# Layer 1's recurrence: inverse matrices kept as 64-column chunk blocks, products as 64x64 blocks

## The chip, the cores and the metric

The kernel runs on one core of a Trainium2 chip. The metric is device time in microseconds of one execution. TensorE is PE in the profile (PEld is its weight load), VectorE is DVE, ScalarE is ACT, GpSimd is POOL.

## The reference

One inference step of a two-layer trunk, for a prompt of 256 tokens and 8 samples of 4 tokens, all in fp32. Layer 0 (SSD heads, sliding-window attention, dense feed-forward) and the mixture of experts behind layer 1 are not touched. The part that matters is the RWKV-7 time mixing of layer 1, 16 heads of width 64:

```python
def step(S, inp):
    r_t, w_t, k_t, v_t, a_t, b_t = inp
    sa = jnp.einsum('bhvk,bhk->bhv', S, a_t)
    S = S * w_t[:, :, None, :] + sa[..., None] * b_t[:, :, None, :] + v_t[..., None] * k_t[:, :, None, :]
    return S, jnp.einsum('bhvk,bhk->bhv', S, r_t)
S1, y = lax.scan(step, wkv0.astype(f32), (tm(r), tm(decay), tm(k), tm(v), tm(-kk), tm(kk * a)))
```

## The kernel before

The scan over 256 tokens is done in four chunks of 64. Inside a chunk the tokens depend on each other through a strictly lower triangular 64x64 matrix per head; the kernel builds the inverse of (1 - that matrix) by doubling, in 6 levels (blocks of 1, 2, 4, ... 32). Two chunks are done at a time as one 128x128 matrix with a block-diagonal mask, so half of each such matrix is zeros. A group g (0 to 3) is a pair of chunks (g // 2) and one half of the heads (8 heads, g % 2).

The order of the work is written out by hand in the list `core`, which every engine walks; `step(name, ...)` appends a step and gives it PSUM banks. The steps of a group:

- X (banks for two row halves): the triangular products of the group, 4 pairs of heads x 2 halves, each with 64 rows contracted and 128 columns. VectorE masks them into `Xt` (L1994).
- M0: VectorE makes the first inverse (level 0 entries plus identity) into `Mti` (L2003, L2005), two ops for each half q of the heads.
- T (g, lv, q): 4 transposes on TensorE (L2777), copied by ScalarE (L1313) from `Mi` to `Mti` (level 0: from `Mti` to `Mi`).
- LY (g, lv, q): 4 products `Xl` x `Mi` of 128x128 (mm, L2317), copied by ScalarE to `Yi` (L1313). `Xl` is `Xt` masked for the level, made by GpSimd (L935, `masked_rows`).
- LM (g, lv, q): 4 products `Mti` x `Yi`, added to `Mi` by VectorE (L2022).
- A (g, p): the score matrices of the pair p of heads, 2 products of 128 columns and 2 of 256; VectorE masks them into `A3` (L2012). There are four A steps a group: behind LM of levels 2 and 4, and around LM of level 5.
- QZ, QU, QY, QS (g, cc): the state part for one chunk cc of the group before, between the steps of the levels: QZ and QU at levels 1 and 3, QY and QS at levels 2 and 4. They use the diagonal blocks of `Mi` and `A3`. QZ opens with products of shape 128*64, the rest of it and QU use one position of the array (64x64); QY and QS alternate between two output halves. ScalarE copies QZ, QU and QY; VectorE updates the state (L2032, L2039).
- Group 0 has no state part; Rv, BO and VT (other projections and transposes) lie between its steps, and VT in group 2.

A level of a later group is therefore, on TensorE: LY 0, T 0, LY 1, T 1, (QZ, or QY and QS), LM 0, LM 1, (QU at levels 1 and 3; A at 2 and 4; X and M0 of the next group at 4). T is that of the level before, and there is none in level 1.

PSUM has 8 banks used in turn: step number modulo 8 gives the bank, `take(g)` waits until the bank's last holder is read, `bank_full` and `bank_free` are its two semaphores. The helper `mm` (L2317) is one matmul call; for fp32 it is two LDWEIGHTS and two MATMUL instructions in the trace, so a step of 4 products has 8.

## Time and profile before

| | |
|---|---|
| median of 3 runs | 1682.53 us (1679.84 to 1685.45) |
| span of the profiled execution | 1682.8 us |
| PE busy in it | 1650.8 us (98%) |
| PEld, DVE, ACT, POOL busy | 1372.4, 1172.6, 915.0, 145.1 us |
| the recurrence's four groups | from about 636 to 797 us |

All numbers are of one profiled execution. A busy PE is not PE at its peak: matmuls are pipelined and their ends are modelled, so the starts of the weight loads tell the pace better than the busy time. "[0.33 <-issue]" behind a row is idle time ahead of it in which the engine waited for nothing that the profile shows.

### The profile page before, as it was taken

The numbers are of one execution on the slowest core, as the hardware profiler recorded it, in microseconds if no ns is written. First come the engines' busy times: TensorE is split into PE (matmuls) and PEld (weight loads), VectorE is DVE, ScalarE is ACT, GpSimd is POOL, SyncE is SP. The second block draws the span as 40 slices with busy tenths as digits, with TensorE's granted clock in tenths as the row PEclk, the third lists the DMA queues.
The fourth block names the chain that finished last, engine by engine and source line by source line (L and its number), as shares of the span: only waits on it lengthen the run. The fifth ranks groups of instructions, "written<-read, shape, count | busy, mean of one in ns | idle before, by whom it ended". The sixth has DMA issues, their size and how long they took to land.

```text
span 1682.8 us, 25536 instructions
## 1 busy us (share of the span) xinstructions
PE 1650.8 (98%) x9976; PEld 1372.4 (82%) x9976; DVE 1172.6 (70%) x1512; ACT 915.0 (54%) x1190; POOL 145.1 (9%) x180
## 2 busy tenths in 40 slices
PE   9999999999999999999999999999999999999999
PEld 7766687999997778998866887878788887878787
DVE  4663732766767645443556979798887979898897
ACT  3352532533427425333435767687776767687774
POOL 1104000000000023222032000000000000000101
PEclk9999889999999999999899999999999999999999
DMA  8922433544423220000156989798997979898993
GB/s 342 390 109 100 201 150 152 225 150 151 150 95 145 101 100 1 2 2 2 58 200 245 427 332 428 313 419 355 377 412 319 428 307 424 347 386 350 380 426 127
DMA packets 41096, 405.02 MB, mean 241 GB/s; under 512 B 4784, under 2 KB 5072, under 8 KB 11664
## 3 DMA queue, kind: packets, MB, share of 16 engines
q1 hardware_dynamic: 34336, 372.64, 54.9%
q0 software_dynamic: 6672, 31.14, 4.6%
q8 instruction: 63, 1.03, 0.2%
q14 instruction: 25, 0.20, 0.0%
HBM read 379.49 MB, written 26.30 MB: 241 GB/s over the span
## 4 chain that ended last, share of the span: by engine, by line
PE 90%; DVE 4%; DMA 2%; ACT 2%; issue 1%; POOL 0%; DVEq 0%; ACTq 0%; SPq 0%; POOLq 0%
PE ps L2317 86%; DMA ring<-in_moe_w 1%; PE ps L3089 1%; PE ps L2777 1%; DVE rest_ring L2124 1%; DMA arena<-in_moe_w 1%; PE ps L2725 1%; DVE arena L1668 0%; ACT arena L1251 0%; DVE arena L1681 0%; ACT arena L1264 0%; PE ps L3042 0%; PE ps L2519 0%; DVE arena L1756 0%; POOL ring L924 0%
## 5 line engine op out<-in xcount | busy, mean ns | idle before, releaser
L2317 PE MATMUL ps<-head,hsel 128*128 128x512 f32 x1408 | 458.1, 397 | 2.8 <-DVE rest_ring L2124 2.8
L2317 PEld LDWEIGHTS ps<-head,hsel 128*128 128x128 f32 x1408 | 264.6, 188 | 61.4 <-DVE rest_ring L2124 7.8
L2124 DVE TENSOR_TENSOR rest_ring<-ring,head 128x2048 fp32r<-128x2048 f32 x128 | 291.1, 2285 | 13.7 <-ACT head L1403 13.7
L2317 PE MATMUL ps<-arena,ring 128*128 128x288 f32 (+9 forms) x1408 | 255.8, 347 | 1.2 <-ACT arena L1257 1.2
L1403 ACT ACTIVATE head<-ring 128x2048 fp32r<-128x2048 f32 x128 | 243.1, 1913 | 20.7 <-DMA ring<-in_moe_w 20.6
L2317 PEld LDWEIGHTS ps<-arena,ring 128*128 128x128 f32 (+4 forms) x1408 | 199.3, 189 | 52.4 <-issue 7.7
L2317 PE MATMUL ps<-rest_ring,hsel 128*128 128x512 f32 x512 | 199.8, 390 | 0.0
L2317 PE MATMUL ps<-head,actT_split 128*128 128x512 f32 x512 | 169.1, 394 | 7.4 <-issue 5.6
L2317 PE MATMUL ps<-rest_arena,head 128*128 128x288 f32 x704 | 174.8, 296 | 0.0
L2317 PE MATMUL ps<-rest_arena,rest_ring 128*128 128x288 f32 x528 | 155.6, 295 | 0.0
L2317 PE MATMUL ps<-h,ring 128*128 128x288 f32 (+2 forms) x624 | 133.5, 371 | 1.8 <-DVE h L1513 1.8
L2317 PEld LDWEIGHTS ps<-h,ring 128*128 128x128 f32 (+2 forms) x624 | 99.6, 176 | 35.3 <-issue 8.9
L2317 PEld LDWEIGHTS ps<-rest_arena,head 128*128 128x128 f32 x704 | 122.6, 188 | 0.1
L2317 PEld LDWEIGHTS ps<-head,actT_split 128*128 128x128 f32 x512 | 96.1, 188 | 31.6 <-issue 8.3
L2118 DVE TENSOR_TENSOR rest_ring<-ring,head 128x2048 fp32r<-128x2048 f32 x48 | 109.7, 2285 | 9.7 <-ACT head L1398 9.6
L2317 PE MATMUL ps<-arena 64*64 64x64 f32 (+11 forms) x1194 | 103.2, 289 | 9.8 <-DVE arena L1701 4.0
L2124 DVE TENSOR_TENSOR rest_arena<-arena,head 128x1024 fp32r<-128x1024 f32 (+1 forms) x64 | 110.3, 1751 | 2.0 <-ACT head L1403 1.7
L2317 PEld LDWEIGHTS ps<-rest_ring,hsel 128*128 128x128 f32 x512 | 96.5, 188 | 18.2
L2317 PE MATMUL ps<-hsel,head 128*128 128x288 f32 x352 | 103.9, 295 | 0.0
L1579 DVE TENSOR_TENSOR x<-x,ps 128x288 f32<-128x288 f32 x110 | 48.2, 452 | 77.7 <-PE ps L2317 77.4
L1403 ACT ACTIVATE head<-arena 128x1024 fp32r<-128x1024 f32 (+1 forms) x64 | 92.5, 1486 | 14.7 <-DMA arena<-in_moe_w 14.5
L2317 PE MATMUL ps<-rest_ring,actT_split 128*128 128x512 f32 x256 | 99.8, 390 | 0.0
(387 smaller groups left out, 2476.0 us busy)
## 6 DMA issues: line engine op xcount, KB each, us to landing
ring<-in_moe_w SPq DMA_DIRECT2D x64, 2048.0 KB, 12.2
ring<-in_moe_w SPq DMA_DIRECT2D x64, 1024.0 KB, 8.2
arena<-in_moe_w SPq DMA_DIRECT2D x24, 2048.0 KB, 11.3
arena<-in_moe_w SPq DMA_DIRECT2D x24, 1024.0 KB, 6.9
ring<-in_ffn_w SPq DMA_DIRECT2D x11, 2048.0 KB, 7.6
ring<-in_ffn_w SPq DMA_DIRECT2D x11, 1024.0 KB, 4.9
moe_rows<-arena POOLq DMA_DIRECT2D x1, 6656.0 KB, 34.0
ring<-in_w_in SPq DMA_DIRECT2D x2, 3072.0 KB, 13.0
```

Of the source, the lines that this page charges most:

```text
L1403: A(mhead[c % 2][:, o:o + w], mslot[s][:, o:o + w], ACT.Copy).then_inc(sem("gu_head"), 1)
L1579: V.tensor_tensor(x[:, m, :], x[:, m, :], bank(g)[:, 0:T], ALU.add).then_inc(freesem(g), 1)
L2118: V.tensor_tensor(mrest[s][:, GU:SLOT], mslot[s][:, GU:SLOT], down_head(c).bitcast(F32), ALU.subtract).then_inc(sem("dn_split"), 1)
L2124: V.tensor_tensor(mrest[s][:, o:o + w], mslot[s][:, o:o + w], mhead[c % 2][:, o:o + w].bitcast(F32), ALU.subtract).then_inc(sem("gu_split" ...
L2317: return nc.tensor.matmul(o, l, r, start=start, stop=stop, skip_group_check=skip)
L2725: ins = nc.tensor.transpose(b[0:rows, i * P:(i + 1) * P], src[:, 4 * hf + i, t0:t0 + rows], ident)
L2777: ins = nc.tensor.transpose(b[:, n * P:(n + 1) * P], (Mi if lv else Mti)[gg % 2][:, 4 * q + n, :], ident)
L3089: ins = nc.tensor.transpose(turned(c)[:, u * P:(u + 1) * P], actm[c % 2][:, u * P:(u + 1) * P], ident)
```

## The change

The matrices `Mi`, `Xt`, `Xl` and `A3` lose their zero halves. Tokens of chunk 0 stay in partitions 0 to 63 and those of chunk 1 in 64 to 127, but a head now has 64 columns and not 128. `Mti` and `Yi` are laid out by pairs of heads: partitions by the head's parity, columns by chunk. Every product of a head and chunk is a 64x64 block, and four of them are issued in turn at the four (row half, column half) positions of the array: (0,0), (1,1), (0,1), (1,0). Products from different row halves go to different banks, so X, A, LY and LM each hold two neighbouring banks with one semaphore (`stage(..., pair=True)`, which rounds the bank up to an even one); LY and LM have 128 columns of each bank.

- LY, LM: 8 products of 64x64 instead of 4 of 128x128. One ScalarE copy or VectorE add of 256 columns over both banks instead of 512.
- T: 2 transposes of 128x128 (two heads in one) instead of 4. Level 0 too goes from `Mi` to `Mti`.
- X: both the product and its transpose, 2 x 16 products of 64x64, instead of 8 of 128 columns. M0 is made from the transposed half straight in PSUM (two VectorE ops of 512 columns), and LY and LM of level 1 wait for M0 alone.
- A: two steps a group (behind LM of levels 2 and 4) of two pairs of heads each, 8 products of 64 columns and 8 of 128; one VectorE op of 768 columns.
- The constant table is narrower (64-column masks).

```diff
-            n = {"X": 2, "A": 2, "M0": 0, ...}.get(name, 1)
-            stage((name, *which), n)
+            n = {"X": 2, "A": 2, "LY": 2, "LM": 2, "M0": 0, ...}.get(name, 1)
+            stage((name, *which), n, pair=name in ("X", "A", "LY", "LM"))
...
                 if lv == 5:
-                    step("A", g, 2)
...
-                    step("A", g, 3)
...
                 elif name == "T":
-                    out_of(g, (Mti if lv else Mi)[gg % 2][:, 4 * q:4 * q + 4, :], bank(g).rearrange("p (h t) -> p h t", t=P))
+                    out_of(g, Mti[gg % 2][:, 2 * q:2 * q + 2, :], bank(g)[:, 0:256].rearrange("p (k t) -> p k t", t=P))
                 elif name == "LY":
-                    out_of(g, Yi[:, 4 * q:4 * q + 4, :], bank(g).rearrange("p (h t) -> p h t", t=P))
+                    out_of(g, Yi[:, 2 * q:2 * q + 2, :].rearrange("p k (c t) -> p c k t", c=2),
+                           banks(g)[:, :, 0:P].rearrange("p c (k t) -> p c k t", k=2))
...
                 elif name == "M0":
-                    for q in range(2):
-                        qs = slice(4 * q, 4 * q + 4)
-                        link(V.tensor_tensor(Mti[gg % 2][:, qs, :], Xt[gg % 2][:, qs, :],
-                                             C("lev0").unsqueeze(1).broadcast_to([P, 4, P]), ALU.mult))
-                        V.tensor_tensor(Mti[gg % 2][:, qs, :], Mti[gg % 2][:, qs, :], idb, ALU.add).then_inc(sem("m0_ready"), 1)
+                    V.tensor_tensor(by_head(Mi[gg % 2], 0, 8), two_banks(gx, 256, 4), masked("lev0u", 4), ALU.mult).then_inc(freesem(gx), 1)
+                    emptied(dve, gx)
+                    V.tensor_tensor(Mi[gg % 2], Mi[gg % 2], C("id64").unsqueeze(1).broadcast_to([P, 8, 64]), ALU.add)\
+                        .then_inc(sem("m0_ready"), 1)
...
                     bs = [take(g), take(g + 1)]
-                    for n in range(4):
-                        i = 4 * hh + n
-                        for q in range(2):
-                            r0 = 64 * q
-                            ins = mm(bs[q][:, n * P:(n + 1) * P], AR[r0:r0 + 64, i, 0, t0:t0 + P], aT[r0:r0 + 64, i, t0:t0 + P])
+                    for turned_ in range(2):
+                        for n in range(4):
+                            i = 4 * hh + n
+                            for cc, q in quarters:
+                                r0, tr, tk = 64 * q, slice(64 * cc, 64 * cc + 64), t0 + 64 * cc
+                                o = 256 * turned_ + 64 * n
+                                l, r = AR[r0:r0 + 64, i, 0, tk:tk + 64], aT[r0:r0 + 64, i, tk:tk + 64]
+                                ins = mm(bs[q][tr, o:o + 64], r, l) if turned_ else mm(bs[q][tr, o:o + 64], l, r)
...
                     b = take(g)
-                    for n in range(4):
-                        ins = nc.tensor.transpose(b[:, n * P:(n + 1) * P], (Mi if lv else Mti)[gg % 2][:, 4 * q + n, :], ident)
+                    for n in range(2):
+                        h0 = 4 * q + 2 * n
+                        ins = nc.tensor.transpose(b[:, n * P:(n + 1) * P], Mi[gg % 2][:, h0:h0 + 2, :].rearrange("p h t -> p (h t)"), ident)
                     done(ins, g)
                 elif name == "LY":
-                    for n in range(4):
-                        ins = mm(b[:, n * P:(n + 1) * P], Xl[:, 4 * q + n, :], Mi[gg % 2][:, 4 * q + n, :])
+                    bs = [take(g), take(g + 1)]
+                    for n in range(2):
+                        for cc, par in quarters:
+                            tr, hd = slice(64 * cc, 64 * cc + 64), 4 * q + 2 * n + par
+                            ins = mm(bs[cc][64 * par:64 * par + 64, n * 64:(n + 1) * 64], Xl[tr, hd, :], Mi[gg % 2][tr, hd, :])
                     done(ins, g)
                 elif name == "LM":
-                    if lv > 1:
-                        emptied(pe, base["T", gg, lv - 1, q])
-                    for n in range(4):
-                        ins = mm(b[:, n * P:(n + 1) * P], Mti[gg % 2][:, 4 * q + n, :], Yi[:, 4 * q + n, :])
+                    emptied(pe, base["T", gg, lv - 1, q])
+                    bs = [take(g), take(g + 1)]
+                    for n in range(2):
+                        for cc, par in quarters:
+                            pr, i = slice(64 * par, 64 * par + 64), 2 * q + n
+                            ins = mm(bs[par][64 * cc:64 * cc + 64, n * 64:(n + 1) * 64], Mti[gg % 2][pr, i, 64 * cc:64 * cc + 64],
+                                     Yi[pr, i, 64 * cc:64 * cc + 64])
```

## Rows read from the trace of the kernel before

**Rows 1.** The page's part 4: the chain that ended last, by engine.
```profile
PE 90%; DVE 4%; DMA 2%; ACT 2%; issue 1%; POOL 0%; DVEq 0%; ACTq 0%; SPq 0%; POOLq 0%
```

**Rows 2.** Windows, a group each: length, busy PE, PEld, DVE, ACT, POOL, clock, DMA, GB/s.
```profile
636.30:672.45 36.15, 35.62 (x293) 32.19 (x293) 18.60 (x29) 19.44 (x38) 13.65 (x13) 1.00 0.00 1
672.45:713.46 41.01, 40.72 (x472) 37.41 (x473) 19.00 (x33) 14.10 (x27) 11.62 (x10) 1.00 0.01 2
713.46:757.11 43.65, 43.25 (x496) 39.95 (x497) 20.52 (x35) 17.25 (x33) 11.53 (x10) 1.00 0.01 2
757.11:797.17 40.06, 38.80 (x448) 35.50 (x449) 13.96 (x26) 13.43 (x25) 8.70 (x8) 1.00 0.01 2
```

**Rows 3.** Groups by line and shape, 620 to 830 us: busy us, mean ns, idle before.
```profile
L2317 PE MATMUL ps<-ring 128*128 128x128 f32 x640 | 84.1, 281 | 1.3 <-issue 1.3
L935 POOL TENSOR_TENSOR ring<-ring,cst 128x512 f32<-128x512 f32 x40 | 45.9, 1154 | 104.1 <-ACT ring L1313 102.4 <-DVEq L1998 1.7
L1313 ACT ACTIVATE ring<-ps 128x512 f32<-128x512 f32 x80 | 44.3, 596 | 48.9 <-PE ps L2317 42.1 <-PE ps L2777 6.8
L2022 DVE TENSOR_TENSOR ring<-ring,ps 128x512 f32<-128x512 f32 x40 | 26.6, 685 | 43.7 <-PE ps L2317 43.4
L2777 PE MATMUL ps<-cst,ring 128*128 128x128 f32 x160 | 23.5, 273 | 0.0
L2032 DVE TENSOR_TENSOR h<-ring,ps 64x256 f32<-64x256 f32 x14 | 5.9, 418 | 36.3 <-PE ps L2317 36.2
L1313 ACT ACTIVATE arena<-ps 128x256 f32<-128x256 f32 x7 | 2.7, 383 | 9.8 <-PE ps L2317 9.8
```

**Rows 4.** Weight loads in order of time, group 2: start, us, operation, [idle before].
```profile
728.27 0.52 PEld L2317 LDWEIGHTS ps<-arena 64*128 64x128 f32 x8
729.12 0.97 PEld L2317 LDWEIGHTS ps<-ring 128*128 128x128 f32 x8 [0.33 <-issue]
730.01 0.47 PEld L2777 LDWEIGHTS ps<-cst,ring 128*128 128x128 f32 x4
...
731.34 0.47 PEld L2777 LDWEIGHTS ps<-cst,ring 128*128 128x128 f32 x4
731.98 0.85 PEld L2317 LDWEIGHTS ps<-ring,arena 128*64 128x64 f32 x8 [0.17 <-issue]
733.00 1.00 PEld L2317 LDWEIGHTS ps<-arena,ring 64*64 64x64 f32 x16 [0.17 <-issue]
734.07 1.86 PEld L2317 LDWEIGHTS ps<-ring 128*128 128x128 f32 x16
736.05 1.00 PEld L2317 LDWEIGHTS ps<-h,ring 64*64 64x64 f32 x16
737.12 0.97 PEld L2317 LDWEIGHTS ps<-ring 128*128 128x128 f32 x8
```

**Rows 5.** Weight loads of small blocks at two positions, in order of time.
```profile
724.27 1.01 PEld L2317 LDWEIGHTS ps<-ring,arena 64*64 64x64 f32 x32
...
726.29 1.86 PEld L2317 LDWEIGHTS ps<-ring 128*128 128x128 f32 x16
...
744.81 1.62 PEld L2317 LDWEIGHTS ps<-arena 64*128 64x128 f32 x24
746.56 0.86 PEld L2725 LDWEIGHTS ps<-cst,arena 128*128 128x128 f32 x8
...
802.23 0.58 PEld L2317 LDWEIGHTS ps<-arena 64*32 64x32 f32 x32
```

**Rows 6.** VectorE in order of time, behind QS of level 2, group 2.
```profile
726.41 0.85 DVE L2032 TENSOR_TENSOR h<-ring,ps 64x256 f32<-64x256 f32 x2 [6.03 <-PE ps L2317]
...
728.18 1.29 DVE L2022 TENSOR_TENSOR ring<-ring,ps 128x512 f32<-128x512 f32 x2
```

**Rows 7.** Windows behind the recurrence, columns as in Rows 2.
```profile
799.00:805.90 6.90, 6.90 (x190) 6.51 (x188) 5.00 (x11) 1.56 (x3) 0.00 (x0) 1.00 0.01 2
...
810.00:815.00 5.00, 5.00 (x59) 5.00 (x59) 1.70 (x4) 0.09 (x1) 0.00 (x0) 0.50 0.00 0
```

More of the change, by code:

```diff
@@ L2310, in take @@
             def take(g):
-                if g >= 8:
-                    pe.wait_ge(freesem(g), g // 8)
+                if before[g] is not None:
+                    emptied(pe, before[g])
                 return bank(g)
```

137 lines of the change are left out of this document (79 added, 58 removed).

## The prediction

> **What bounds the kernel now.** The chain that ended last is TensorE for 90% of the span [rows 1]; the question is whether that also holds in the stretch that the change touches. The windows over the four groups of layer 1's recurrence answer it: of 160.9 us between 636.3 and 797.17, TensorE is busy 158.4 us, and VectorE, ScalarE and GpSimd are busy 72, 64 and 45 us [rows 2]. DMA moves next to nothing there. So a microsecond of TensorE taken out comes off the time, until a chain through the other engines shows. Look next at one level (group 2, level 3): its weight loads follow each other without idle time that is not a change of shape [rows 4]. The start-to-start times of that view are the prices below; a matmul of fp32 is two instructions, so a step of 4 products of 128x128 is 8 of them.
>
> **Prices from the rows.** A product step now takes 0.89 us (LY, 729.12 to 730.01), 8 instructions of 128 columns at 111 ns; two LY and a T fill 729.12 to 731.34, so T costs 2.22 - 2 x 0.89 = 0.44, 4 transposes at 110 ns [rows 4]. Sixteen instructions of 64 columns that all sit at one position take 1.07 us (736.05 to 737.12). Every block that ends in a change of array shape shows a surplus over columns: LM 734.07 to 736.05 is 1.98 for 16 x 0.111 = 1.78, T before QZ 0.64 for 0.44. I take 0.18 a change; then the 16 instructions at one position cost 0.89, 56 ns each [rows 4]. Next, QY and QS: 64 instructions of 64x64 whose output alternates between two halves, 724.27 to 726.29, 2.02 - 0.18 = 1.84, so 28.7 ns each: half [rows 5]. X alternates between the two row halves: X and A together take 1.75 us (744.81 to 746.56), A alone 0.85 (728.27 to 729.12), so X is 0.90 for 16 instructions of 128 columns, 56 ns instead of 111 [rows 4, 5]. Two positions overlap in both directions.
>
> **What four positions are worth.** No row of before uses four, so this is bounded: from below 14.4 ns (a quarter of 57, all four overlapping), from above 56 ns (a diagonal pair doesn't overlap at all). I take 28.7. Matmuls start in program order, and each product is two instructions at the same position, the second of which can start only when the first has streamed. With order a1 a2 b1 b2 c1 c2 d1 d2, b1 can start beside a2 but b2 must wait one full stream for b1. That gives one pair per 57 ns however many positions there are, which is also what the two-position rows show. Two of the four orders of neighbours (rows change alone, columns change alone) are those rows; the diagonal step is the one that isn't shown.
>
> **The change, part by part**, on TensorE:
> - LY and LM, 80 steps: 8 instructions at 111 ns become 16 at 28.7, 0.89 to 0.46: 80 x 0.43 = 34.4 us off.
> - T, 40 steps: 4 transposes become 2, 0.44 to 0.22: 8.8 off.
> - X, 4 steps: 16 instructions of 128 columns (0.90) become 64 of 64 (64 x 28.7 = 1.84), since the transposed product is now made too: 3.8 on.
> - A: 16 steps of 0.85 - 0.18 = 0.67, in all 10.7; now 8 steps of 16 x 28.7 + 16 x 56 ns = 1.36, in all 10.9: nothing.
> - Changes of shape. Between LY and T there were none; now T (128x128) sits between 64x64 blocks, 3 more in each of the 16 levels that have T's; but LM to QU, QZ to LM, QS to LM, LM to A and QU to LY become the same shape. Counted through a group of 1 to 3 this is 22 before and 21 after; group 0, which has no Q steps, goes from 8 to 22. Net +11 x 0.18 = 2.0 on.
> Sum: 34.4 + 8.8 - 3.8 - 0.2 - 2.0 = 37.2 us of TensorE less.
>
> **Idle time that goes, and that comes.** TensorE's idle time in the four groups is 0.5 + 0.3 + 0.4 + 1.3 = 2.5 us [rows 2]. At a group's start LY waited for T's copy by ScalarE, and in group 3 QZ waited for VectorE's masking of the last A. Now LY waits for M0 alone, and the A's are done by level 4: I take 2.2 back. What is late next is the chain of a level. The evacuations shrink: ScalarE's copy of 512 columns (596 ns) becomes 256 (383 ns, the 128x256 row), VectorE's add 685 ns becomes about 420 (the 64x256 row), GpSimd's rows 1154 ns become perhaps 750, M0 is two ops instead of four and A is evacuated once a pair [rows 3]. A level without other work between: LY0 ends at 0.46, copy from 0.72 to 1.10; T0's copy to 1.5, LY1's to 2.1, T1's to 2.56; TensorE reaches LM0 at 2.06 and LM1 at 2.52, so LM1 waits 0.15 for T1's copy. VectorE's add of LM0 ends 0.9 us after LM0's last issue and gates the next LY0, 0.45 behind LM1; only group 0 has such levels (VT, A or X lies in most), and I charge it 1 us. In levels 2 and 4 VectorE does the state ops first, 1.77 us from 726.41 to 728.18, before LM's add [rows 6]: QS ends at 4.74 into the level, adds begin at 6.8, LY0 of the next level may start at 7.4, TensorE is there at 7.0 behind A: 0.4 lost in level 2 of groups 1 to 3 and in level 4 of group 3 (elsewhere X covers it), 1.7. With 0.15 in three fifth levels: 3.2 us of new idle time. GpSimd needs 2 x 0.75 us a level of at least 3.4 and is let go by LY's copy, so it waits for others, as now. Banks: a step now holds two and pads to an even one, so a bank comes round after four to six steps instead of eight; the nearest case is T of level 4 behind X, whose banks M0 still reads, and they free at the moment TensorE comes. Nothing, and 0.5 us for each of 3 if I am wrong.
> Constants shrink by some 0.4 MB of a load of 1501 KB near the start; nobody waits for it in the chain: nothing, at most 1 us off.
>
> Net: 37.2 + 2.2 - 3.2 = 36.2 us. The profiled execution has a span of 1682.8 us and the runs' median is 1682.53, so the one stands for the other: 1682.5 - 36.2 = 1646. Everything behind 797 us is released by TensorE's own progress through the stage, so the gain reaches the end.
>
> **Rivals.**
> (1) All four positions overlap: 14.4 ns. Then 1664 instructions of 64 columns (80 x 16 + 256 + 128) save 14.3 ns more each, 23.8, and A's 128 of 128 columns 28 ns, 3.6. But levels 2 and 4 then hang on VectorE's 7 us chain and level 5 on ScalarE's copies, so about 18 of 27 arrive: 1628. For it: 32 instructions of 32 columns, at two row positions in turn, take 0.58 us, 18 ns each, so starting instructions isn't the limit at 28.7 [rows 5]. Against it: the order of pairs above. The Trainium skill, TensorE: Matmul & The Clock Gate, Part 3 (Packing small matmuls), has tiles of different positions start 4 ns apart, so four products would take the time of one; by that the time is that of this rival. The rows of two positions fit both readings. Chance 0.12.
> (2) The short blocks don't amortise their changes of shape: if each of the 48 new LY/T changes and the 14 of group 0 costs 0.38 instead of 0.18 (idle marks of 0.33 us at the change behind A [rows 4]), 12 us go back: 1658. Chance 0.17.
> (3) The four positions don't overlap across the diagonal, or at all: 56 ns. Then LY and LM cost 0.90 each, as now, and 1664 x 27.3 ns = 45.4 and 128 x 55 ns = 7.0 come on top of 1646, less the 3.2 of idle time that is then covered: 1695, slower. It decides from 50 ns an instruction upward: 36.2 / (1664 + 128) = 20 ns over mine. Against it: both kinds of two-position rows [rows 4, 5]. A rule that speaks against the change: the Trainium skill, same page, section Wait — 56ns, not 53.3ns?, says that with hardware decode off the sequencer spends about 62 ns per matmul, which binds when array work is shorter; by that the time would be near this rival's. This trace shows 18 ns between starts, so the measurement decides against it. Chance 0.06.
> (4) The granted clock falls to 1.2 GHz while small blocks run. It fell in this trace: full in 799 to 805.9, where blocks of 64x64 and 64x32 fill the array, and 0.50 in 810 to 815, after 128 matmuls of 16 columns each [rows 7]. In the changed stage the columns stream without a break except for changes of shape, so 799 to 805.9 is the nearer row. At half the clock each microsecond of work costs one more: the kernel is slower than before from 36 us of the stage's 120 at the low level; all of it would be 1750. Chance 0.06 for that much.
> (5) The change does all it says but the saving is not on the path, because another engine set the pace: excluded but for 0.01 by the busy sums [rows 2].
>
> **How the numbers follow.** Forecast 1646 (0.58), its own range 1638 to 1654 (A and LY stalls of 0.15 more a level on one side, 26 ns an instruction and the constants on the other). Rival 1: 0.12, rival 2: 0.17, rivals 3 and 4: 0.12 together, rest 0.01. The range for 8 in 10 takes in rivals 1 and 2: 1625 to 1662. Faster by over 0.3% (5 us, about what runs of this kernel can tell from no change): 0.87; within 0.3%: 0.02 (rival 4 in part of the stage, and rival 5); slower: 0.11.
>
> **What would show it.** In the profile after: LY and LM steps of 16 instructions of 64x64 spanning 0.46 us start to start (0.23 for rival 1, 0.9 for rival 3); T steps of two at 110 ns with 0.18 us idle ahead of the next block (0.38 for rival 2); X 1.84 us; group 1 from its first LY to the next group's 30.8 us instead of 41.0; VectorE's state ops as what releases LY behind level 2; clock 1.00 in the whole stage. The prediction is wrong if small blocks leave gaps that the columns don't explain, or if levels come out at over 3.5 us where nothing lies between.

## The result and the profile after

| | before | after |
|---|---|---|
| median | 1683.99 us (1679.84 to 1686.09, 4 runs) | 1639.95 us (1637.31 to 1643.72, 4 runs) |
| span of the profiled execution | 1682.8 us | 1634.3 us |
| mean granted clock in it | 0.989 | 0.987 |

The ratio is 0.9743, with a 95% interval of 0.9727 to 0.9759: 44 us less by the medians, 48.5 by the two profiled executions. The forecast was 36.2 less, 1646. So sign and place came out, and the time lies in the forecast's own range of 1638 to 1654. The rest of this text is about two terms that were both too small and partly cancelled: what four positions are worth, and the idle time that a faster TensorE meets.

**The chain.** Part 4 of the page of after, the answer to [rows 1]:

```profile
PE 88%; DVE 5%; ACT 2%; DMA 2%; issue 2%; POOL 0%; DVEq 0%; ACTq 0%; SPq 0%; POOLq 0%
```

**The four groups.** Windows of after, from each group's first LY to the next group's, the last up to the first QZ of group 3, with the columns of [rows 2]:

```profile
636.05:661.57 25.52, 21.69 (x513) 17.12 (x512) 11.03 (x22) 14.54 (x37) 7.06 (x11) 1.00 0.01 3
661.57:689.46 27.89, 24.54 (x694) 21.32 (x693) 10.83 (x24) 9.79 (x27) 6.70 (x10) 1.00 0.01 3
689.46:719.35 29.89, 27.34 (x717) 24.00 (x716) 10.76 (x24) 12.41 (x32) 6.78 (x10) 1.00 0.01 4
719.35:745.75 26.40, 22.97 (x625) 19.84 (x625) 8.52 (x19) 9.92 (x27) 4.96 (x8) 1.00 0.01 3
```

Set beside [rows 2]: the stage took 160.9 us and takes 109.7, 51.2 less. TensorE's busy time fell by more than that, from 158.4 to 96.6 (61.8), and its idle time rose from 2.5 to 13.2 us. Where 40.7 of 41.0 us of group 1 were busy, 24.5 of 27.9 are now.

**The price of a block.** Weight loads of after in order of time (start, us, operation, idle before), which answer [rows 4, 5]: X(0), then T(2,1,0), LY(2,2,1) and T(2,1,1) with QY behind it:

```profile
625.60 1.02 PEld L2342 LDWEIGHTS ps<-arena 64*64 64x64 f32 x64 [0.39 <-issue]
626.69 1.27 PEld L2342 LDWEIGHTS ps<-arena,ring 128*128 128x128 f32 x6
...
694.57 0.20 PEld L2809 LDWEIGHTS ps<-cst,ring 128*128 128x128 f32 x2
694.94 0.32 PEld L2342 LDWEIGHTS ps<-ring 64*64 64x64 f32 x16 [0.17 <-issue]
695.33 0.20 PEld L2809 LDWEIGHTS ps<-cst,ring 128*128 128x128 f32 x2
695.50 0.97 PEld L2342 LDWEIGHTS ps<-arena,ring 128*128 128x128 f32 x8
```

X is 64 instructions (here and below: matmuls, each with a weight load of its own) in 1.09 us to the next block; less 0.17 for the change of shape that is 0.92, 14 ns each. LY, 16 instructions, reaches the T behind it in 0.39, or 0.22 without the change: 14 ns again. T takes 0.17 with no change behind it (695.33 to 695.50) and 0.37 with one (694.57 to 694.94). The forecast had 28.7 ns for X, LY, LM and for half of A's instructions.

These 14 ns are a mean and not the distance between two starts. The matmuls of LY(0,2,0) start at 0, 7, 14 and 20 ns, at 107, 114, 120 and 127, at 165, 172, 179 and 185, and at 224, 230, 237 and 244 ns: four almost together, one for each position, and, from the second round on, a round every 58 ns. Cut off at 643.53 us, the view holds the first round alone:

```profile
643.43 0.29 PE L2342 MATMUL ps<-ring 64*64 64x64 f32 x4
```

**The other engines**, grouped by line and shape over 620 to 790 us, the answer to [rows 3] (busy us, mean ns, idle before):

```profile
L2342 PE MATMUL ps<-ring 64*64 64x64 f32 x1280 | 34.7, 227 | 9.8 <-DVE ring L2047 5.1 <-issue 3.3 <-DVE ring L2027 0.6
L1332 ACT ACTIVATE ring<-ps 128x256 f32<-128x256 f32 x80 | 27.2, 386 | 27.2 <-PE ps L2342 24.4 <-PE ps L2809 2.6
L954 POOL TENSOR_TENSOR ring<-ring,cst 128x256 f32<-128x256 f32 x40 | 26.5, 675 | 76.6 <-ACT ring L1332 69.2 <-DVE ring L2023 7.0
L2047 DVE TENSOR_TENSOR ring<-ring,ps 128x256 f32<-128x256 f32 x40 | 15.5, 418 | 33.4 <-PE ps L2342 33.1
```

The copy and the add cost what the prediction said, 386 ns for 383 and 418 for 420; GpSimd's rows take 675 for 750. The last number of the first line is the news: LY and LM, which had waited 1.3 us in all, wait 9.8, and 5.1 of it is for VectorE's add (L2047).

**VectorE behind level 2** of group 2, the answer to [rows 6], and the TensorE rows that wait for it:

```profile
698.67 0.85 DVE L2057 TENSOR_TENSOR h<-ring,ps 64x256 f32<-64x256 f32 x2 [4.85 <-PE ps L2342]
699.55 0.85 DVE L2064 TENSOR_TENSOR ring<-h,arena 64x256 f32<-64x256 f32 x2
700.44 0.75 DVE L2047 TENSOR_TENSOR ring<-ring,ps 128x256 f32<-128x256 f32 x2
```

```profile
698.87 0.67 PEld L2342 LDWEIGHTS ps<-arena 64*64 64x64 f32 x32
700.93 0.35 PEld L2342 LDWEIGHTS ps<-ring 64*64 64x64 f32 x16 [1.39 <-issue]
```

QS ends, VectorE makes the two halves of the state's update (0.85 each) and only then LM's adds; TensorE has meanwhile done LM and A(2,0) and stands 1.39 us. The same gap, 1.37 to 1.42 us, stands behind level 2 of groups 1 to 3 and behind level 4 of group 3 (at 672.96, 700.93, 730.87 and 742.99), and half a microsecond of it before level 5 of group 1 (685.24). The rest of the 13.2 us: level 5 with its banks and a stall in group 0 (both below), LM's waits in group 0, and six waits of QU for QZ's copy that were covered before (0.35 to 0.52 us on the weight loads, 1.9 us in all on the matmuls).

**Behind the stage** the lead was 51.4 us at the first QZ of group 3 and is 48.5 at the end. Windows behind that QZ, first of before, then of after, at equal distance from it, answer [rows 7]:

```profile
807.17:822.17 15.00, 15.00 (x145) 13.05 (x143) 9.33 (x16) 5.30 (x14) 0.00 (x0) 0.55 0.01 3
837.17:852.17 15.00, 14.54 (x149) 10.27 (x148) 5.73 (x13) 6.15 (x11) 2.96 (x3) 1.00 0.52 198
```

```profile
755.75:770.75 15.00, 15.00 (x145) 12.72 (x143) 9.33 (x16) 5.64 (x14) 0.00 (x0) 0.56 0.00 1
785.75:800.75 15.00, 14.55 (x140) 10.47 (x140) 5.01 (x9) 6.15 (x11) 2.05 (x2) 0.89 0.54 204
```

The dip of the clock to 0.55 that stood behind the stage is still there (0.56). The first difference is the second row of each pair: 0.89 for 1.00. That is a low clock for 3.4 us from 795 us on, which costs 1.7. Another microsecond stands ahead of the first experts' products, where TensorE waits 1.15 and 1.10 us for VectorE (L2307) instead of 0.83 and 0.34. ScalarE's waits for the experts' weights by DMA also grew (20.6 to 24.9 us in all on the one ring), but that these are the cause of it is not shown.

### The profile page after: what moved, and what is told of

The parts are those of the page before. It is cut to its first block, busy times and chain, and to the rows that moved or that the text cites. A ratio compares the mean times of both kernels' runs of the same rounds, so it can differ in the third digit from the quotient of the medians.

```text
span 1634.3 us, 27320 instructions
## 1 busy us (share of the span) xinstructions
PE 1590.1 (97%) x10856; PEld 1309.2 (80%) x10856; DVE 1137.9 (70%) x1476; ACT 896.8 (55%) x1190; POOL 123.3 (8%) x180
## 3 DMA queue, kind: packets, MB, share of 16 engines
q8 instruction: 70, 1.15, 0.3%
## 4 chain that ended last, share of the span: by engine, by line
PE 88%; DVE 5%; ACT 2%; DMA 2%; issue 2%; POOL 0%; DVEq 0%; ACTq 0%; SPq 0%; POOLq 0%
PE ps L2342 85%; DMA ring<-in_moe_w 1%; PE ps L3127 1%; DMA arena<-in_moe_w 1%; DVE rest_ring L2149 1%; PE ps L2809 1%; PE ps L2750 1%; DVE arena L1688 0%; ACT arena L1270 0%; DVE arena L1701 0%; ACT arena L1283 0%; PE ps L3080 0%; PE ps L2544 0%; DVE h L2057 0%; DVE arena L1776 0%
## 5 line engine op out<-in xcount | busy, mean ns | idle before, releaser
L2149 DVE TENSOR_TENSOR rest_ring<-ring,head 128x2048 fp32r<-128x2048 f32 x128 | 291.0, 2284 | 14.4 <-ACT head L1423 14.3
L1423 ACT ACTIVATE head<-ring 128x2048 fp32r<-128x2048 f32 x128 | 243.1, 1912 | 24.9 <-DMA ring<-in_moe_w 24.9
L2342 PEld LDWEIGHTS ps<-h,ring 128*128 128x128 f32 (+2 forms) x624 | 99.6, 176 | 37.6 <-issue 10.7
L2143 DVE TENSOR_TENSOR rest_ring<-ring,head 128x2048 fp32r<-128x2048 f32 x48 | 109.7, 2285 | 9.7 <-ACT head L1418 9.7
L2149 DVE TENSOR_TENSOR rest_arena<-arena,head 128x1024 fp32r<-128x1024 f32 (+1 forms) x64 | 110.3, 1750 | 3.7 <-ACT head L1423 3.5
L2342 PE MATMUL ps<-arena 64*64 64x64 f32 (+13 forms) x1514 | 96.9, 266 | 9.9 <-DVE arena L1721 4.0
```

What stands on the lines that cost most here:

```text
L1423: A(mhead[c % 2][:, o:o + w], mslot[s][:, o:o + w], ACT.Copy).then_inc(sem("gu_head"), 1)
L2143: V.tensor_tensor(mrest[s][:, GU:SLOT], mslot[s][:, GU:SLOT], down_head(c).bitcast(F32), ALU.subtract).then_inc(sem("dn_split"), 1)
L2149: V.tensor_tensor(mrest[s][:, o:o + w], mslot[s][:, o:o + w], mhead[c % 2][:, o:o + w].bitcast(F32), ALU.subtract).then_inc(sem("gu_split" ...
L2342: return nc.tensor.matmul(o, l, r, start=start, stop=stop, skip_group_check=skip)
```

## The experiments

Three questions: why four positions cost 14 ns and not 28.7; what holds TensorE up now; and why runs of one kernel spread by 10 us and more. All ratios are to the kernel before.

**e1 and e2: the order of the positions.** The kernel after goes (0,0), (1,1), (0,1), (1,0) for every product. In LY, LM and X, e1 makes all products at the first two positions in turn and then those at the other two; e2 all of one position in a row, then the next. A stays as it was.

```
-  for n in range(2):
-      for cc, par in quarters:
+  for n, cc, par in in_turn(2):      # and in_turn(4) in X
   # e1: for duo in (quarters[0:2], quarters[2:4]) for n for c, r in duo
   # e2: for c, r in quarters for n
```

> The changed kernel with the products of LY, LM and X in another order: all products of the positions (0,0) and (1,1) first, in turn, then all of (0,1) and (1,0). Nothing else moves; A keeps its four in turn. Theory P (positions run beside each other, one stream of 64 columns each, 57 ns, shared by as many positions as are visited in turn): 28.7 ns an instruction instead of 14, so LY and LM steps of 16 instructions take 0.46 us start to start instead of 0.23, X 1.84 instead of 0.92. TensorE work 80 x 0.23 + 4 x 0.92 = 22 us more, of which the idle time of levels 2, 4 and 5 swallows some 10: 1650, and in any case near the 1646 that was forecast with this price. Theory Q (a position has a deep queue of its own, the order of issue doesn't matter): unchanged, 1640 and 14 ns.

Measured: 1635.51 us median, ratio 0.9711 (0.9647 to 0.9775), span 1632.8.

> The changed kernel with the products of LY, LM and X ordered by position: all of (0,0), then all of (1,1), and so on, so 4 instructions in a row (8 in X) go to one position. Theory P: only the last instruction of a position and the first of the next run beside each other, so 45 to 57 ns an instruction: LY and LM 0.75 to 0.9 us, X 3.2 to 3.6; TensorE work 45 to 60 us more than with four in turn, ten of it swallowed by idle time: 1675 to 1690, so about what the kernel before takes. Theory Q: unchanged, 1640.

Measured: 1634.90 us median, ratio 0.9701 (0.9642 to 0.9759), span 1631.7. X(0) of e1, then of e2:

```profile
623.26 1.43 PEld L2342 LDWEIGHTS ps<-arena 64*64 64x64 f32 x64 [0.39 <-issue]
```

```profile
623.11 2.55 PEld L2342 LDWEIGHTS ps<-arena 64*64 64x64 f32 x64 [0.39 <-issue]
```

LY and LM cost the same in both as in the kernel after: 0.34 us for 16 weight loads against 0.32 to 0.35. In e2 a position there gets four instructions in a row. X, where it gets eight in a row, costs 2.55 us instead of 1.02; in e1, where two positions share a row of sixteen, 1.43. So for LY and LM theory Q holds and theory P falls, and for X neither. The prediction's argument (matmuls start in program order, and the second instruction of a product holds up everything behind it) would have put LY of e2 at or above 0.46; it falls.

The single starts show what happens instead. In e2's LY four matmuls start within 40 ns, though the first four of the program all sit at one position: the positions start out of program order, each as soon as its first instruction has come through. Their distances are 13 ns in e2 (four instructions a position), 7 in the kernel after (two), and 7, 20 and 7 in e1, so 3.3 ns for each matmul that stands between. In e2's X the starts are 0, 106, 165, 223 and 281 ns, and then 287: the second position begins 6 ns behind the fifth start of the first, and the later positions follow at steps of 288 ns, five times 57.6. First e2's LY, cut off at 642.68 us, then its X, cut off at 623.39:

```profile
642.58 0.31 PE L2342 MATMUL ps<-ring 64*64 64x64 f32 x4
623.11 0.50 PE L2342 MATMUL ps<-arena 64*64 64x64 f32 x5
```

So while a position works on one instruction, three more can wait for it; in a row of eight the last one gets its place when the fifth starts, and only then is the next position reached. That gives (7 x 5 + 8) x 57 ns = 2.45 us for X of e2, where 2.55 are measured, and (3 x 5 + 8) x 57 ns = 1.31 for e1, where 1.43 are measured. The records don't name the position; this is read from the order of the starts and these two sums.

**e6: two positions only.** LY and LM issue the same number of instructions, but only at (0,0) and (1,1), twice each. The products of the other two positions are left out, and the copies of LY and QU are scaled by zero.

```
+  two = ((0, 0), (1, 1), (0, 0), (1, 1))
-      for cc, par in quarters:       # in LY and in LM
+      for cc, par in two:
```

> LY and LM issue as many instructions of the same shape, but all at the positions (0,0) and (1,1) in turn: the products of (0,1) and (1,0) are left out, and those of the two others are made twice (the copies of LY and QU are scaled by zero so that no number grows; the instructions stay). Theory L (one position takes 57 ns for a 64-column instruction, and positions run beside each other): 28.7 ns an instruction, LY and LM 0.46 us each, which is the price that the prediction put on four positions. Then the rest of the prediction's sum can be read: group 1 should take the 30.8 us forecast, and the whole 1646 us, some 8 to 15 us more than the kernel after. Rival S (the array starts an instruction of this shape every 14 ns wherever it sits, as long as neighbours differ): 14 ns, 0.23 us a step, and the time of the kernel after, 1640. Rival N (the diagonal pair does not overlap): 57 ns, 0.9 us a step, group 1 near 40 us and the whole near 1680.

Measured: 1643.54 us median, ratio 0.9762 (0.9723 to 0.9801), span 1641.2. Its windows of the four groups, and an LY with its T:

```profile
636.05:662.26 26.21, 25.46 (x513) 21.26 (x512) 11.68 (x22) 14.75 (x37) 7.20 (x11) 1.00 0.01 3
662.26:692.07 29.81, 28.51 (x693) 25.75 (x692) 11.02 (x24) 10.37 (x27) 6.67 (x10) 1.00 0.01 3
692.07:724.25 32.18, 31.09 (x717) 28.21 (x717) 10.94 (x24) 13.15 (x32) 6.80 (x10) 1.00 0.01 3
724.25:752.65 28.40, 26.92 (x626) 24.26 (x625) 8.69 (x19) 10.45 (x27) 5.05 (x8) 1.00 0.01 3
```

```profile
644.31 0.54 PEld L2342 LDWEIGHTS ps<-ring 64*64 64x64 f32 x16 [0.17 <-issue]
644.92 0.20 PEld L2810 LDWEIGHTS ps<-cst,ring 128*128 128x128 f32 x2
```

LY to T is 0.61 us less 0.17 for the change: 0.44, 28 ns an instruction. Theory L holds: a position takes 57 ns for a 64-column instruction, and two positions give 28, four give 14. This kernel has the price that the prediction put on LY and LM, so the rest of its sum can be read off: group 1 takes 29.8 us (forecast 30.8) and the stage 116.6. The forecast for the stage was 160.9 - 36.2 = 124.7. The 8.1 us between are 9.2 less of busy time (112.0 instead of 158.4 - 37.2 = 121.2), which is X and A at four positions (9.2 too, below), and 1.1 more of idle time (4.6 instead of 3.5). The gap behind level 2 is 0.95 us here. And the run measures what the better price was worth. 80 steps x 16 x 14.3 ns are 18.3 us of TensorE, of which 15.4 show as busy time (112.0 against 96.6); the stage of the kernel after is 116.6 - 109.7 = 6.9 us shorter for it, and so are the two spans. The ratios differ by 0.0019, 3.2 us, and their intervals don't tell that from nothing. Rival 1 was right on the price, and right that part of it would not arrive; it kept 18 of 27 where, of the stage, 15 of 27 came. Its time of 1628 is farther from the measured 1640 than the forecast's 1646 is.

**e3 and e5: the state's update.** e3 moves QY and QS of levels 2 and 4 behind LM on all engines; e5 leaves TensorE's order and lets VectorE do LM's two adds before QS.

```
   if g:
       if lv in (1, 3): state_part(g - 1, lv // 2, 0)
-      elif lv in (2, 4): state_part(g - 1, lv // 2 - 1, 2)
   for q in range(2): step("LM", g, lv, q)
+  if g and lv in (2, 4): state_part(g - 1, lv // 2 - 1, 2)      # e3
+  walk: QS, LM, LM -> LM, LM, QS, for VectorE alone             # e5
```

> The changed kernel with QY and QS behind LM in levels 2 and 4 (for every engine), so that VectorE adds LM's result before it updates the state. Theory D (the idle time of 1.4 us at the LY behind level 2, and behind level 4 of group 3, is VectorE's state update in front of LM's add): 4 such places and two of 0.3 to 0.5 go, 6.3 us; but QY and QS no longer lie between T and LM, where LM then waits for ScalarE's copies, about 0.5 in 6 places, 3 us back: 1636 to 1638. Rival: the copies' wait eats all of it, or the masking of X and M0, now later, holds the fifth level: 1640 or more.

Measured: 1641.98 us median, ratio 0.9727 (0.9663 to 0.9792), span 1640.5.

> The changed kernel with one thing moved on VectorE alone: in levels 2 and 4 it does the two adds of LM before the state update of QS; TensorE's order is as it was. Theory D: the LY behind is released by the add some 1.4 us earlier. But LY's banks in level 3 are those of QS and of the LY before it (the bank round is short now that a step holds two), so it waits for the first half of the state update, which comes 0.9 us behind the adds: 0.3 to 0.5 us gained in each of 4 places, 1638 to 1640. If banks don't matter: 4 x 1.2, 1635. If idle time doesn't move at all the add wasn't the reason.

Measured: 1644.81 us median, ratio 0.9733 (0.9667 to 0.9800), span 1649.0. Neither time can be told from that of the kernel after. Groups 2 and 3 decide, which ran at full clock in these profiles (group 1 did not: the clock was at 0.50 for 6.8 us in e3 and for 20.5 us in e5). They take 31.0 and 27.3 us in e3, 30.6 and 27.1 in e5, and 29.9 and 26.4 in the kernel after: both orders are slower by 0.7 to 1.1 us a group. In e3 the gap ahead of LY goes and one of 1.26 us comes ahead of the T behind it, which waits for the masking of A(g,0) (L2036). In e5 the gap behind level 2 stays (1.21 us) and a new one comes at X:

```profile
693.60 1.02 PEld L2346 LDWEIGHTS ps<-arena 64*64 64x64 f32 x64 [1.04 <-DVE h L2061]
```

X takes the PSUM bank that QS's update (L2061 here) has not yet freed. Both theory D's gain and e5's forecast of 1638 to 1640 us missed.

**e12: the update split.** VectorE makes the half that frees the bank where it did, and the product with the decay behind LM's adds.

```
-  QS: add; product with decay; LM: add; LM: add
+  QS: add; LM: add; LM: add; QS2: product with decay
```

> VectorE makes the two halves of QS's evacuation apart: the add that frees the bank ahead of the adds of LM, as now, and the product with the decay behind them. Theory D (LY behind level 2 and level 4 waits for VectorE's chain of add, product, add of LM): the 1.4 us ahead of LY behind levels 2 and 4 falls to 0.6 in groups 1 to 3, and nothing that moving the whole (1.04 us ahead of X for QS's bank) had cost comes in its place: some 5 x 0.8 = 4 us off the span at the same clock. Rival: QZ of level 3, A or X then waits for the later product (state or bank), 0.5 us or more, and the groups keep 27.9, 29.9 and 26.4 us.

Measured: 1640.16 us median, ratio 0.9719 (0.9688 to 0.9749), span 1647.3. The gap before LY falls from 1.4 to 0.5 us, but T(g,2,1) of the same level then waits 1.0 us: it takes the bank of A(g,0), whose masking (954 ns) now stands behind the product. Groups 2 and 3 take 29.9 and 26.5 us, as the rival had it. The split is in e13 too, and there the same level reads (weight loads, then TensorE's own row for that T):

```profile
669.69 0.35 PEld L2358 LDWEIGHTS ps<-ring 64*64 64x64 f32 x16 [0.53 <-issue]
...
671.82 0.20 PEld L2825 LDWEIGHTS ps<-cst,ring 128*128 128x128 f32 x2 [1.01 <-ACT ring L1339]
```

```profile
671.85 0.41 PE L2825 MATMUL ps<-cst,ring 128*128 128x128 f32 x2 [0.91 <-DVE ring L2050]
```

Three ways of ordering, one result. VectorE has 0.85 + 0.85 + 0.75 + 0.95 = 3.4 us to do between QS and the next bank that TensorE wants, and whichever piece is last takes the wait. That the gap behind level 2 is VectorE's is shown; that an order of the same work could remove it is refuted for these three. An order that was not tried, A's masking ahead of the product with the decay, stays open.

**e4, e7, e8: banks, and the transposes together.** e4 leaves two numbers out of the round of banks ahead of T(g,4,1) in groups 0 and 1 and ahead of LY(2,5,1). e7 orders a level LY LY T T. e8 is e3 and e4 together.

```
+  if lv == 5 and q and g == 2: order[0] += 2       # e4, ahead of LY
   step("LY", g, lv, q)
+  if lv == 5 and q and g < 2: order[0] += 2        # e4, ahead of T
   if lv > 1: step("T", g, lv - 1, q)               # e7: a loop of its own behind both LY
```

> Two numbers are left out of the round of PSUM banks ahead of T(g,4,1) in groups 0 and 1 and ahead of LY(2,5,1), so that the steps of level 5 take other banks than X's, which VectorE's M0 still reads. Theory B (the waits of 0.6 us in level 5 are waits for X's banks): the idle time ahead of LY(g,5,1) and T(g,4,1) of groups 0 to 2 (0.58, 0.62 and 0.56 us in the kernel after) goes to under 0.2, groups 1 and 2 are 0.5 us shorter each (27.9 to 27.4, 29.9 to 29.4), the span 1.5 to 2 us shorter. Rival W (those steps were only early, and LM of level 5 waits for the evacuations of M0 and of LY in any case): the idle time moves to LM of level 5 and the groups keep their 27.9 and 29.9 us.

Measured: 1637.18 us median, ratio 0.9713 (0.9669 to 0.9757), span 1635.9. TensorE's rows from LY(2,5,0) on, first of the kernel after, then of e4:

```profile
714.24 0.46 PE L2342 MATMUL ps<-ring 64*64 64x64 f32 x16
714.63 0.44 PE L2809 MATMUL ps<-cst,ring 128*128 128x128 f32 x2
715.63 0.46 PE L2342 MATMUL ps<-ring 64*64 64x64 f32 x16 [0.56 <-DVE ring L2027]
```

```profile
715.78 0.46 PE L2346 MATMUL ps<-ring 64*64 64x64 f32 x16
716.17 0.44 PE L2813 MATMUL ps<-cst,ring 128*128 128x128 f32 x2
716.68 0.46 PE L2346 MATMUL ps<-ring 64*64 64x64 f32 x16
```

The wait for M0 (L2027) is gone, and group 2 takes 29.22 us instead of 29.89. The wait of T(1,4,1), 0.73 us, is gone too. That of LY(1,5,1) stayed at 0.58: its matmul row names VectorE's L2040, the masking of A(1,1) (L2036 in the kernel after). So theory B is right for X's banks, and that step waits for a bank of A's. The span did not get shorter (1635.9 for 1634.3): the clock was at 0.50 for 6.8 us from 659.4 on.

> The order inside a level becomes LY LY T T instead of LY T LY T. Theory C (a change between 64x64 blocks and T costs TensorE 0.18 us each time, and TensorE is what sets the pace): two changes less in each of 16 levels, 32 x 0.18 = 5.8 us off, of which some 3 arrive, because LY(q=1) comes 0.36 us sooner behind the adds and LM(q=0) now waits for T(q=0)'s copy, the third of four instead of the second. Rival E (the levels are set by the evacuations, not by TensorE's changes): TensorE's busy time falls by 5 us and its idle time grows by as much; the same time within 1 us, or 1 to 3 us longer, since the copy that LM(q=0) waits for is 0.39 us later.

Measured: 1637.93 us median, ratio 0.9706 (0.9656 to 0.9757), span 1638.3. By its time it can't be told from the kernel after. The T's do stand together (four transposes, 0.42 us), but the gaps ahead of LM grow to 1.2 us in group 0, and the clock was at 0.50 for 20.5 us behind it. Groups 2 and 3, at full clock again but for 0.9 us at the end, say more: 28.69 and 25.36 us instead of 29.89 and 26.40. Theory C has 8 changes of 0.17 to 0.18 us less in a group, 1.4; 1.2 and 1.0 came. So theory C is right in these two groups. In group 0, whose end lies in the low clock, the gaps ahead of LM took the gain back (25.5 us, as in the kernel after).

> QY and QS behind LM in levels 2 and 4, and the two numbers of banks left out, both. Theory D with B (LY behind level 2 waits for VectorE's state update ahead of the adds, level 5 for X's banks): the 1.4 us ahead of LY behind level 2 falls under 0.5 in groups 1 to 3 (4 us), the 0.6 us of level 5 goes (2 us): groups 1 to 3 are 26.0, 28.0, 25.0 us where the kernel after has 27.9, 29.9, 26.4, a span of 1628 to 1630. Rival: the update of the state is only moved, X or the next QZ waits for it or for its bank, and the groups keep 27 to 29 us; the whole stays within 2 us of 1640.

Measured: 1637.53 us median, ratio 0.9718 (0.9677 to 0.9758), span 1642.3. Groups 2 and 3 take 30.2 and 27.3 us against e4's 29.2 and 26.3: the late QS costs a microsecond a group here as well. A span of 1628 to 1630 was expected; the clock was at 0.50 for 6.8 us of this one's stage, but the groups at full clock miss their 28.0 and 25.0 us too.

**e10: a stall that belongs to the place in the program.** In the kernel after, LY(0,5,0) issues two instructions and then stands 1.73 us with no releaser. The only thing that moves near it is one transfer on the instruction queue. Weight loads of after, then windows around the transfer (the last number is GB/s):

```profile
654.40 1.73 PEld L2342 LDWEIGHTS ps<-arena 64*64 64x64 f32 x96
656.01 0.19 PEld L2342 LDWEIGHTS ps<-ring 64*64 64x64 f32 x2
657.93 0.32 PEld L2342 LDWEIGHTS ps<-ring 64*64 64x64 f32 x14 [1.73 <-issue]
```

```profile
655.30:655.35 0.05, 0.05 (x19) 0.05 (x13) 0.00 (x0) 0.00 (x0) 0.00 (x0) 1.00 1.63 328
655.35:657.90 2.55, 0.93 (x64) 0.85 (x57) 2.47 (x4) 0.00 (x0) 0.00 (x0) 1.00 0.00 0
```

From the transfer's start to the end of the stall it is 2.63 us. In the other kernels the pair moves together: 653.50 and 656.16 in e1, 654.45 and 657.24 in e2, 655.25 and 657.85 in e3, 655.30 and 657.95 in e4, 655.75 and 658.18 in e6, 654.75 and 657.18 in e7, and so in e5, e8, e12 and e14: always 2.4 to 2.8 us. The stall itself is 1.25 to 2.01 us long in nine of these profiles, and 0.43 in e2 and 0.16 in e6, whose X or LY give TensorE more time. In all of them it stands at the same matmul, the 4330th of the execution. And the transfers keep step with TensorE's program: each is 16384 bytes, and from one to the next TensorE executes 256 weight loads and matmuls in the mean of the first 66 (8462, 8794, 9006 and 9230 are done at 649.0, 655.3, 659.9 and 664.6 us). e10 makes X(0)'s products twice, which moves everything behind by 64 matmuls and their 64 weight loads in the program and changes no bank and no order.

```
-  for turned_ in range(2):
+  for turned_ in ((0, 1, 0, 1) if which[0] == 0 else (0, 1)):
```

> X(0) makes its 64 products twice, so that every later instruction of TensorE stands 64 instructions further on in its program; nothing else is changed. In the kernel after, LY(0,5,0) stalls for 1.73 us after its first two instructions with nothing that releases it, 2.6 us after a transfer of 16 KB on the instruction queue; five other kernels with that stall or a weaker one end it 2.4 to 2.8 us after their own such transfer. Theory F (the stall is TensorE running out of its program: the transfer brings the next piece, and blocks at 14 ns an instruction use up what is left before it is there): the transfer near X(1) comes 64 instructions sooner against the work (beside the start of A(0,1) instead of the middle of X(1)), and the stall moves 64 instructions forward, into the middle of X(1) or A(0,1), again ending 2.4 to 2.8 us after the transfer's start; none is left in LY(0,5,0), and the one of 0.58 us ahead of LY(1,5,1) moves too. The time is that of the kernel after and 0.9 us. Rival W (LY(0,5,0) waits for a bank, a buffer or another engine): the stall stays in LY(0,5,0) at 1.7 us and LY(1,5,1) keeps its 0.58.

Measured: 1636.32 us median, ratio 0.9710 (0.9684 to 0.9736), span 1636.7, with 64 matmuls and 64 weight loads more than the kernel after. Its weight loads at the same place:

```profile
653.99 1.78 PEld L2342 LDWEIGHTS ps<-arena 64*64 64x64 f32 x96
655.64 0.36 PEld L2342 LDWEIGHTS ps<-ring 64*64 64x64 f32 x16
```

The stall is gone from LY(0,5,0), and group 0 takes 23.80 us instead of 25.52, which is the stall's 1.73. The transfer now starts at 652.05, 1.9 us ahead of this block instead of in its middle, and the next one at 655.85. So rival W falls: the stall hangs on where instructions stand in the program. That TensorE runs out of its program there is the reading that fits, the transfers of 256 instructions each with it. Theory F was not right in its detail: it had the stall reappear inside X(1), and there is none. It reappears a group later: X(2) stands 0.62 us with 16 of its matmuls to go, until 2.8 us behind the transfer at 680.30. The 0.58 us ahead of LY(1,5,1) is another thing, the wait for VectorE's masking of A(1,1) of e4. It became 0.42 because that step comes later behind the new stall.

**e13 and e14: the kernel after again, and three edits together.** e13 has e12's split, e4's spread of banks (in group 0 a level earlier), and X(1) with M0(1) behind level 3 of group 0, so that A(0,1) and X(1) no longer stand in a row. e14 is the kernel after, unchanged, on the same chip.

```
+  if lv == 3 and g == 0: step("X", 1); step("M0", 1)
   if lv == 4:
       step("A", g, 1)
-      if g < 3:
+      if 0 < g < 3:
           step("X", g + 1)
```

> Three edits at once: the split of the state update, the numbers left out of the round of banks so that nothing near the fifth level takes X's banks, and X(1) with M0(1) behind level 3 instead of level 4 in group 0, so that A(0,1) and X(1), 96 instructions at 14 ns, do not stand in a row. Theories D, B and F together: 4 us by the split, 1.3 by the banks, 1 to 1.7 by the missing stall of group 0, and where the stall is gone the granted clock stays 1.00 in group 1 (it fell to 0.50 there for 8 us in four of the five profiles with that stall of 1.7 us, which costs some 3 us): a span of 1626 to 1629, a median 6 to 9 us under the kernel after of the same call. Rival: the waits are one chain and take turns: the whole stays within 3 us of the kernel after.

Measured: 1630.76 us median (1628.94 to 1635.38, 5 runs), ratio 0.9690 (0.9669 to 0.9711), span 1628.2.

> The changed kernel itself, unchanged, on the same chip as the three others, so that a few microseconds can be told: 1640 us. Theory K (the granted clock falls after the stall of group 0 in some of its executions and not in others): if this profile shows the stall of 1.73 us near 656 us and a clock of 0.50 behind it, group 1 takes 29 us instead of 27.9 and the span is 1637 or more; the records of the first profile showed 1.00 there. Rival: the same instructions get the same clock each time: 1.00 again, and the lower clock of the variants was due to their edits.

Measured: 1646.07 us median (1637.64 to 1652.31, 6 runs), ratio 0.9767 (0.9740 to 0.9794), span 1645.1. Windows of 4 us around the end of group 0 (PE busy is the second number, the granted clock the third from the right), first of the kernel after, then of e14, then of e13:

```profile
656.00:660.00 4.00, 2.24 (x71) 1.60 (x62) 2.31 (x4) 1.55 (x5) 0.76 (x2) 1.00 0.02 4
660.00:664.00 4.00, 3.45 (x79) 2.88 (x73) 0.84 (x2) 1.79 (x6) 1.75 (x3) 1.00 0.00 0
```

```profile
656.00:660.00 4.00, 2.08 (x51) 1.48 (x43) 2.27 (x4) 1.13 (x4) 0.64 (x1) 0.82 0.00 0
660.00:664.00 4.00, 4.00 (x71) 2.96 (x71) 0.84 (x2) 2.18 (x6) 0.64 (x1) 0.50 0.01 4
```

```profile
656.00:660.00 4.00, 3.25 (x89) 2.35 (x89) 1.56 (x3) 3.03 (x10) 1.27 (x2) 1.00 0.02 4
660.00:664.00 4.00, 3.58 (x83) 3.31 (x87) 0.75 (x2) 0.89 (x3) 1.23 (x2) 1.00 0.01 4
```

Theory K holds. The same program, with nearly the same stall (1.73 us, and 2.01 in e14), had its clock at 1.00 in one execution and at 0.50 for 6.8 us in the other, and the two levels are 2.4 and 1.2 GHz. The stage of e14 is 2.3 us longer, 0.3 of it the longer stall itself. It loses 8.5 more behind: the first 10 us behind the last group run at a clock of 0.70 instead of 1.00, and a later stretch of 75 us at 0.89. Over all the profiles, a fall of the clock to 0.50 within 3 us follows the stall in seven of the nine executions in which it was 1.25 us or longer (e3, e4, e5, e7, e8, e12 and e14, for 6.8 or 20.5 us; not in the kernel after and in e1), and in none of the four with 0.43 us or less of it (e2, e6, e10, e13). That makes the stall a likely cause, not a sufficient one: the gaps of 1.4 us behind level 2 stand in the kernel after at full clock.

In e13, where TensorE stands less in 656 to 660, the clock stays 1.00 throughout the stage. Its stage is 741.87 - 636.01 = 105.9 us, 3.8 less than after's. Of that 2.4 us are group 0, 0.6 group 1, 0.8 group 2 and 0.1 group 3. So by its place the missing stall is worth most, the banks some, and the split little; e4 and e12 have two of the edits alone, but the move of X(1) was not run alone. The lead of 15 us over e14 by the medians, where 6 to 9 were expected, is more than the 3.8 us of work. By the two profiled spans it is 16.9 us: 3.8 of work in the stage, 10.8 that e14's execution lost against the kernel after's, most of it by the clock, and 2.3 behind the stage. e13 beats both kernels: 1630.76 against 1646.07 us on the same chip, intervals of the ratio apart.

## Why the prediction came out as it did

It was right in place, sign and, by its own range, in size. Of its mechanism, what bounds the stage and what would wait next were right; the argument under its largest price was not, and that the total still came out within 6 us is partly luck, as the sum below shows. Step by step:

- **What bounds the kernel.** Right: a microsecond of TensorE came off the time until other chains showed.
- **LY and LM, 0.89 to 0.46 us.** The mis-sized term. They are 0.22 to 0.25, 14 ns an instruction [rows 5 had 28.7 for two positions]. The step that failed is the argument of the pairs (matmuls start in program order, so b2 must wait for b1 before c1 can start); e2's starts refute it, and e6 shows what the two-position rows did mean: 57 ns a position, divided by the positions in use. Worth 18.3 us more of TensorE.
- **X, +3.8 us.** Without the change behind it, it was 0.92 us a time instead of 1.84: 4 x 0.92 = 3.7 us less than charged. **A, nothing:** 32 instructions take 0.67 us (648.02 to 648.69 in e6) where 1.36 was charged: 8 x 0.69 = 5.5 us more off. The same term again, 9.2 us together, and 9.2 is what e6's busy time shows.
- **T, 0.44 to 0.22; a change of shape 0.18.** Right: 0.17 to 0.22, and 0.17. Rival 2's 0.38 a change falls: T with a change behind it is 0.37 in all.
- **Idle time, -2.2 and +3.2.** Too small by about 10 us: 13.2 us stand where 3.5 were forecast. The mechanism behind levels 2 and 4 was named with its engine and order; its size was 1.4 us instead of 0.4 because TensorE's side was priced too high. e6 shows the steps: with LY and LM at the forecast's price, but A 0.69 us cheaper than it, the gap is 0.95, and in the kernel after the two LM take 0.44 us less again. A chain of another engine has a fixed length, so each microsecond by which the bound engine's work was overrated is missing in the forecast of its waits.
- **Banks: nothing, 0.5 us each for three if wrong.** It was wrong: 0.73, 0.56 and 0.61 (LM(0,5,1)), and e4 took them away. A fourth, 0.58 ahead of LY(1,5,1), is for a bank of A's and stayed.
- **What the prediction did not list:** QU behind QZ's copy, 1.9 us in all, and the stall behind the instruction transfer, 1.73.
- **The clock (rival 4).** Taken as all or nothing, 0.06. It comes in part: absent from the stage in the first profile, 2 us in the stage of e14 and 8.5 behind it. The recorded 1750 for the whole stage at half clock is too low by its own sum: 121 us of work would make it 1767.
- **Rival 2's 12 us** count the changes of group 0 twice, since the 48 of 16 levels hold them already; without them it is under 10. It didn't come, so nothing hangs on it.

The sum: 37.2 + 18.3 + 9.2 = 64.7 us less of TensorE by the corrected prices (61.8 of busy time measured), less 10.7 of new idle time, is 54 in the stage by the prices (51.2 measured), less 3 behind it. The forecast of 36.2 was nearer than its terms because the price and the idle time erred in opposite directions; nothing in its argument made them do so, and that is luck.

The Trainium skill, TensorE: Matmul & The Clock Gate, Part 3 (Packing small matmuls — row/col tiling), has tiles that work at the same time and start some 4 ns apart, and matmuls that start and end in program order. The trace agrees with the first: the four positions start 7 ns apart with two matmuls each, 3.3 ns a matmul, and rival 1's price is the measured one. It does not agree with the order of the starts, which the prediction leaned on: in e2's LY the second position starts 13 ns behind the first, ahead of three matmuls that stand before it in the program. The same page's section Wait — 56ns, not 53.3ns? has 62 ns a matmul with hardware decode off; X at 14 ns a matmul lies far under that, and no run here shows which decoding was on.

Open: why the stall's transfer starts no earlier, whether three waiting instructions a position is the limit for other shapes too, and why the clock falls in one execution and not in another of the same program.

## What to carry to other kernels

Price a packed block by the time of one position divided by the number of positions in use, and check that with a row for two before arguing about order; keep rows at one position short (four here). When the bound engine gets cheaper, write down the length of each other engine's chain between two of its steps and compare it with the new, not the old, pace: the gain stops there, and in three orders tried here the wait only moved. Very dense blocks of small instructions are best not set in a row. An idle gap can go with a loss through the clock behind it that is larger than the gap, so read the granted clock of each profile before comparing two of them, and compare stretches at the same clock.

## What was not expected of the hardware

- TensorE most likely can run out of its program. With 112 matmuls at 14 ns in a row, each with its weight load (A(0,1), X(1) and the start of LY(0,5,0)), it stood 1.25 to 2.01 us in nine profiles, always at the same matmul and until 2.4 to 2.8 us after the start of a transfer of 16384 bytes on the instruction queue. Moving the program by 128 instructions took the stall away from there, and 1.7 us off the group.
- A position takes 57 ns for a 64-column fp32 instruction whatever the others do: 28 ns with two in use, 14 with four. The positions do not start in program order: one instruction is at work and three more can wait at each, at 3.3 ns apiece. In a row of four at one position nothing is lost, in a row of eight (X of e2) 2.55 us instead of 1.02.
- With the same program and nearly the same gap the granted clock stayed 1.00 once and fell to 0.50 for 6.8 us another time. Over the six runs of e14 the mean clock goes from 0.974 to 0.985 while the time goes from 1652.31 to 1637.64 us.
